# Decoder trunk on one core: up-projection panels taken in pairs, three products split once more, and four of the inner weight sums made on VectorE

## What is computed

```python
def swiglu(u, w_up, w_down):
    h = u @ w_up
    a, b = jnp.split(h, 2, axis=-1)
    return (jax.nn.silu(a) * b) @ w_down

u = rmsnorm(x, ng[0]) * (1.0 + sc1) + sh1
x = x + 0.5 * g1 * swiglu(u, P['w_ffn_up'][l, 0], P['w_ffn_down'][l, 0])
```

## Time and profile before

| | us |
|---|---|
| median of 3 runs | 3175.61 |
| lowest and highest | 3175.28 to 3176.03 |
| the profiled execution | 3176.12 |
| its span in the trace | 3174.4 |
| TensorE busy | 3132.2 |
| VectorE busy | 1169.0 |
| GpSimd busy | 856.6 |

### The profile page before, as it was taken

One profiled execution on the slowest core, in us unless ns is written; L12 is line 12 of the kernel. 1 busy time (PEld: TensorE's weight loads), 2 busy tenths in 40 slices (PEclk: granted clock), 3 DMA queues, 4 the chain that ended last, 5 costly groups with the idle time before them and its releaser, 6 DMA issues.

```text
span 3174.4 us, 42750 instructions
## 1 busy us (share of the span) xinstructions
PE 3132.2 (99%) x17722; PEld 2483.5 (78%) x17722; DVE 1169.0 (37%) x2229; ACT 421.1 (13%) x806; POOL 856.6 (27%) x749
## 2 busy tenths in 40 slices
PE   7999999999999999999999999999999999999999
PEld 5777887678777878888877778876787778788887
DVE  3223432453233463344232233224533244633432
ACT  2000001212111120000010000023021111200000
POOL 2333431210000334334333334302100003344442
PEclk9999999999999999999999999999999999999999
DMA  6544323541111223332234443234311113222221
GB/s 244 196 174 171 127 74 107 161 136 40 51 51 58 90 79 115 112 112 81 86 120 170 176 169 116 74 119 147 126 53 51 34 58 106 77 80 80 80 83 65
DMA packets 73504, 337.43 MB, mean 106 GB/s; under 512 B 10592, under 2 KB 27744, under 8 KB 40288
## 3 DMA queue, kind: packets, MB, share of 16 engines
q1 hardware_dynamic: 63936, 312.03, 27.1%
q0 software_dynamic: 6816, 18.88, 2.0%
q10 hardware_dynamic: 2560, 3.80, 0.3%
HBM read 326.55 MB, written 6.02 MB: 105 GB/s over the span
## 4 chain that ended last, share of the span: by engine, by line
PE 97%; DVE 2%; ACT 1%; DMA 1%; issue 0%; SPq 0%; DVEq 0%; ACTq 0%
PE ps L702 96%; DVE ws L1729 1%; ACT ws L1450 0%; DMA lp<-params 0%; ACT u L1450 0%; DMA ring<-w_ada 0%; DVE u L1729 0%; DVE proj L1729 0%; DVE masked_room L2104 0%; PE ps L762 0%; DVE x L1732 0%; PE ps L1277 0%; DVE masked_room L1729 0%; DVE masked_room L1732 0%; PE ps L1164 0%
## 5 line engine op out<-in xcount | busy, mean ns | idle before, releaser
L702 PE MATMUL ps<-u,ring 128*128 128x272 f32 x4608 | 1145.4, 398 | 10.9 <-ACT u L1450 9.3
L702 PEld LDWEIGHTS ps<-u,ring 128*128 128x128 f32 x4608 | 858.1, 190 | 227.3 <-issue 45.6
L1729 DVE TENSOR_TENSOR ws<-ws,ps 128x272 f32<-128x272 f32 (+2 forms) x778 | 346.6, 451 | 1488.9 <-PE ps L702 1482.1
L665 POOL TENSOR_TENSOR masked_room<-ring 128x512 f32<-128x512 f32 (+1 forms) x76 | 95.8, 1260 | 1277.9 <-DVE pause L2430 651.6
L702 PE MATMUL ps<-y,ring 128*128 128x272 f32 x1376 | 350.8, 393 | 0.0
L1450 ACT ACTIVATE ws<-ps 128x272 f32<-128x272 f32 (+1 forms) x398 | 154.9, 396 | 1316.0 <-PE ps L702 1315.4
L702 PE MATMUL ps<-y,masked_room 128*128 128x272 f32 x1296 | 315.9, 393 | 2.8 <-DVE ws L1729 2.8
L702 PE MATMUL ps<-y,ws 128*128 128x272 f32 x1296 | 315.7, 393 | 0.0
L702 PEld LDWEIGHTS ps<-y,ring 128*128 128x128 f32 x1376 | 261.4, 190 | 54.3 <-DVE proj L1729 0.7
L702 PEld LDWEIGHTS ps<-y,masked_room 128*128 128x128 f32 x1296 | 245.6, 190 | 55.7 <-issue 5.3
L702 PEld LDWEIGHTS ps<-y,ws 128*128 128x128 f32 x1296 | 246.0, 190 | 51.9 <-issue 1.6
(11 more groups left out here) (201 smaller groups left out, 2543.4 us busy)
## 6 DMA issues: line engine op xcount, KB each, us to landing
ring<-w_up SPq DMA_DIRECT2D x88, 1024.0 KB, 4.8
ring<-w_ada SPq DMA_DIRECT2D x72, 1024.0 KB, 4.8
ring<-w_down SPq DMA_DIRECT2D x32, 1024.0 KB, 4.7
ring<-w_gate SPq DMA_DIRECT2D x32, 1024.0 KB, 4.8
ring<-w_in SPq DMA_DIRECT2D x22, 1024.0 KB, 4.8
ws<-cache SPq DMA_DIRECT2D x128, 128.0 KB, 3.1
ws<-cache POOLq DMA_DIRECT2D x128, 128.0 KB, 3.4
ring<-w_down SPq DMA_DIRECT2D x16, 768.0 KB, 4.1
```

The lines of the kernel that those rows point to most:

```text
L665: nc.gpsimd.tensor_tensor(sums[:, 0], a21, a22, ALU.add).then_inc(w_sums.sem, 1)
L702: return nc.tensor.matmul(out, lhsT, rhs, start=start, stop=stop, skip_group_check=skip)
L1729: return V.tensor_tensor(out, a, b, op)
```

## The change

Panels 0, 1 and 18 to 21 stay as they were. The 16 between become 8 pairs (r = 1 to 8, `PAIRS`). In a pair eight products stay as they are, with both panels' M1, M2, M5 and M3 (a, b). The other three (six, seven, four, the old M6, M7 and M4 of both panels) are each taken as one product of 512 x 256 weights against 512 x 272 tokens, and that is split once more: seven inner products of 256 x 128 against 256 x 136, 2 matmuls each. Each is done in a front (four inner products) and a rear (three), with one of the eight products between.

- The inner token sums are made once a feed-forward by GpSimd (`inner_token_sums`, 12 instructions, into `proj`).
- The weight sums S1 to S4 of both panels (8 instructions of 512 elements a pair) and the inner weight sums of six and seven (4 of 256 elements each) are made by GpSimd (`pair_block_sums`). S3 and S4 are written over parts of the panel in the ring.
- The inner weight sums of four, the product with raw weights, are made by VectorE (`raw_sums`, 4 instructions of 256 elements), ordered behind step seven and ahead of the adds of M5.
- VectorE adds each split product together with seven instructions (`step`) and writes hidden values two tiles at a time.
- A modulation panel no longer takes a slot of the ring: it has a room of its own (`side`), and its matmuls stand at four places of a pair. Chunks are done in pairs 1 to 7 (f = 0) and in pairs 2 and 3 of the first layer's f = 1.
- A ring slot of a pair is free when its M3 has ended, no longer after that product's first matmul.
- The first hidden sums are made during the last four panels, four instructions in each.

The core of the diff:

```diff
+                def pair_block_sums(f, r):
+                    blocks = pair_blocks(f, r)
...
+                        pair_sums(pool, l, f, r - 1, "S4b")
+                    pair_sums(pool, l, f, r, "S1b")
+                    for a, (a11, a12, a21, a22) in enumerate(blocks):
+                        nc.gpsimd.tensor_tensor(pair_s2[:, a], pair_s1[:, r % 2, a], a11, ALU.subtract)\
+                            .then_inc(pr_pool.sem, 1)
+                    pair_sums(pool, l, f, r, "S2b")
+                    inner_sums(f, r, "6", [in6[:, i] for i in range(4)], pair_s2[:, 0], pair_s2[:, 1])
...
+                    for a, (a11, a12, a21, a22) in enumerate(blocks):
+                        nc.gpsimd.tensor_tensor(a21, a11, a21, ALU.subtract).then_inc(pr_pool.sem, 1)
...
+                        pair_pe(pool, l, f, r - 1, "7.3")
+                    pair_sums(pool, l, f, r, "S3b")
+                    inner_sums(f, r, "7", [inner_room(in7, i) for i in range(4)], blocks[0][2], blocks[1][2])
...
+                        pair_pe(pool, l, f, r - 1, "4.3")
+                    if r < PAIRS:
+                        first_pair_sums(f, r + 1)
+                    for a, (a11, a12, a21, a22) in enumerate(blocks):
+                        pair_pe(pool, l, f, r, ("M2a", "M2b")[a])
+                        nc.gpsimd.tensor_tensor(a12, a12, pair_s2[:, a], ALU.subtract).then_inc(pr_pool.sem, 1)
```

```diff
+                    side_modulation(l, f, r, 1)
+                    pair_sums(pe_, l, f, r, "7s4")
+                    pair_dve(pe_, l, f, r, "6.7")
+                    seven_[0]()
...
+                    side_modulation(l, f, r, 2)
+                    pair_dve(pe_, l, f, r, "4s4")
+                    if first:
+                        pe_.wait_ge(in_sums.sem, in_sums.upto(l, 12 * f + 12))
+                    pair_dve(pe_, l, f, r, "7.7")
+                    four[0]()
+                    pair_sums(pe_, l, f, r, "S4a")
+                    pair_dve(pe_, l, f, r, "c22_a")
+                    plain(2, raw(0, 4, 0), tok(4, HALF), False, part)
+                    four[1]()
+                    side_modulation(l, f, r, 3)
+                    pair_sums(pe_, l, f, r, "S4b")
+                    pair_dve(pe_, l, f, r, "c22_b")
+                    plain(5, raw(1, 4, 0), tok(4, HALF), False, part)
```

```diff
+                    def raw_sums(r):
+                        slots = [panel_wait(dve, l, f"up{n}", 2 * r + a) for a in range(2)]
+                        (top0, top1), (low0, low1) = [
+                            [ring[:, s, :].rearrange("p (k m) -> p k m", k=8)[:, k:k + 2, P:256] for k in (4, 6)]
+                            for s in slots]
+                        room = [inner_room(in4, i) for i in range(4)]
...
+                            pair_pe(dve, l, n, r - 1, "4.3")
+                        tt_(room[0], low0, low1, ADD).then_inc(pr_dve.sem, 1)
+                        tt_(room[2], top0, low0, SUB).then_inc(pr_dve.sem, 1)
+                        pair_dve(dve, l, n, r, "4s1")
+                        tt_(room[1], room[0], top0, SUB).then_inc(pr_dve.sem, 1)
+                        pair_dve(dve, l, n, r, "4s2")
+                        tt_(room[3], top1, room[1], SUB).then_inc(pr_dve.sem, 1)
...
+                    step("7", pair_second, pair_third)
+                    before = chunk_of(l, n, r - 1)
...
+                        keep_modulation(l + n, before)
...
+                    raw_sums(r)
+                    pair_dve(dve, l, n, r, "7.7")
+                    for a in range(2):
+                        pair_pe(dve, l, n, r, ("M5a", "M5b")[a])
+                        tt_(half(pair_c22, a), half(pair_third, a), ps[:, 2 + 3 * a, 0:HALF], ADD).then_inc(pr_dve.sem, 1)
```

More of the change, by code:

```diff
@@ L163, with single, singles, chunk_of @@
[L163 to L169, removed]
+PAIRS = 8
+SINGLE = FT - 2 * PAIRS
+QUARTER = HALF // 2
+def single(q):
+    return q if q < 2 else q - 2 * PAIRS
+def singles():
+    return [q for q in range(FT) if q < 2 or q >= 2 + 2 * PAIRS]
+def chunk_of(l, f, r):
+    if f == 0:
+        return r + 1 if 1 <= r <= 7 else None
+    return r - 2 if l + 1 < DEPTH and r in (2, 3) else None
@@ new lines, in side_number @@
+def side_number(l, f, r, k):
+    before = [(a, b, c) for a in range(DEPTH) for b in range(2) for c in range(1, PAIRS + 1)
+              if (a, b, c) < (l, f, r) and chunk_of(a, b, c) is not None]
+    return CHUNK * len(before) + k + 1
+PAIR_PE = {n: i + 1 for i, n in enumerate(
+    ("M1a", "M1b", "6.1", "6.2", "M2a", "6.3", "M2b", "7.1", "7.2", "M5a", "7.3", "M5b", "4.1", "4.2", "4.3"))}
+PAIR_ACT = {n: i + 1 for i, n in enumerate(("first_a", "first_b", "gate1_a", "gate1_b", "gate2_a", "gate2_b"))}
@@ L672, in weight_sums @@
                 def weight_sums(f):
-                    for q in range(FT):
+                    for q in singles():
                         if f and q == 0:
@@ L777, in ffn @@
                             sum_squares(l, 0)
-                        modulation(l, panel(l, "ada", n), n)
+                        modulation(l, ring[:, panel(l, "ada", n), :], n, part)
                         if n % CHUNK == CHUNK - 1:
@@ L790, in product @@
                     m.then_inc(wi_pe.sem, 1)
-                for q in range(FT):
-                    place, unit, sums_at = up_place(l, f, q), f * FT + q, 4 * unit_of(f"up{f}", q)
+                for q in singles():
+                    place, unit, sums_at = q, f * SINGLE + single(q), 4 * unit_of(f"up{f}", single(q))
+                    if q == 2 + 2 * PAIRS:
+                        for r in range(1, PAIRS + 1):
+                            pair(r)
                     s = load_number(l, f"up{f}", place) % R
@@ L1901, in products @@
+                for q in singles():
+                    if q == 2 + 2 * PAIRS:
+                        for r in range(1, PAIRS + 1):
+                            pair(r)
+                    unit, by, bz = n * SINGLE + single(q), 3 * (q % 2) + 1, 3 * (q % 2) + 2
                     def products(k):
```

358 lines of the change are left out of this document (284 added, 74 removed).

## The result

| | before | after |
|---|---|---|
| median of the runs, us | 3175.82 | 3285.47 |
| lowest to highest, us | 3175.28 to 3177.51 | 3270.27 to 3293.79 |
| profiled execution, us (span) | 3176.1 (3174.4) | 3293.79 (3292.1) |
| mean granted TensorE clock, profiled | 0.998 | 0.979 |

The changed kernel takes 1.0338 times as long (95% interval 1.0309 to 1.0366), 110 us more. Forecast were 83 us more, 3258.6 us, with a range of 3200 to 3315. Its runs spread far more than those of before, and the spread follows the granted clock: 3270.27 us at 0.987, 3285.80 at 0.982, 3285.13 at 0.981, 3293.79 at 0.979.

What follows compares the result with a forecast made beforehand. The prediction took TensorE's own pace to bound the kernel. Its terms -40 (split), +3 (modulation panels), +100 (wait for the four sums) and +20 (clock) gave +83 on 3175.6, so 3258.6 us, range 3215 to 3315 with turns.

Steps and rivals of the forecast that it cites:

- Part 1: Inner split of three products a pair, 136-column records at 116 ns each: TensorE work falls by 40 us.
- Rival (d): 136-column records cost TensorE what 272-column ones do: +264 in place of -40, about 3440 us; chance 0.03.
- Part 2: Modulation panels in their own buffer: single panels cost +3 us, late side loads 0 (bound 32 us).
- Part 3: VectorE's extra adds and GpSimd's extra sums stay hidden behind TensorE's products: no cost.
- Part 4: Four front waits for VectorE's four weight sums, slowed by turns with GpSimd: +100 us, bounds 27 and 135.
- (a): VectorE's four sums don't meet GpSimd's: 3166 us, or 3138 if TensorE doesn't wait at all; chance 0.12.
- (b): VectorE waits one turn, then keeps GpSimd out until all four sums are through: 3177 us; chance 0.05.
- Rival (c): Turns, but cheaper: the four sums fall on GpSimd's short inner sums, no clock loss: 3202 us; chance 0.09.
- Part 5: TensorE's granted clock falls to half after waits ahead of four front: +20 us, bounds 0 and 48.

Runs made afterwards that it cites:

- e7_gpsimd_loads: Changed kernel with four's inner weight sums made by GpSimd, and mask and parameter loads moved from panel 12 to 18: 3142.97 us.
- e2_start: Changed kernel with VectorE's four sums moved to the pair's start, ahead of step six: 3152.59 us, ratio 0.992 to the kernel before.
- e3_yield: Changed kernel with GpSimd held from the next pair's sums until VectorE's fourth sum is there: 3171.76 us, ratio 0.9982 to the kernel before.
- e5_middle: Changed kernel with VectorE's four sums moved between step six and step seven: 3153.91 us, ratio 0.9927 to the kernel before.
- e6_start_loads: e2_start with the mask and parameter loads moved from panel 12 to panel 18: 3143.49 us, ratio 0.9896 to the kernel before.

## Why the prediction was right, point by point

The sign, the place and the mechanism were right and the time fell in the range; forecast were +83, measured +110 (median) and +118 (the profiled execution). By its own steps, for the profiled execution:

| step | forecast, us | measured, us | read from |
|---|---|---|---|
| 1 inner split | -40 | -40 | 136-column records |
| 2 modulation singles | +3 | +3 | not measured by itself |
| 2 side panels late | 0 | +5 | waits for `ws<-w_ada` |
| 3 more adds and sums hidden | 0 | 0 | no other wait |
| 4 wait for the four sums | +100 | +93 | how late the 32 four fronts are |
| 5 clock | +20 | +57 | what remains; 56 read behind the gaps |

**Part 1** holds: eight 136-column records start between 2895.63 and 2896.56, 0.116 us each, the value taken. That the split pays is shown by e7_gpsimd_loads, where 34 of the 37 us are there. Rival (d) falls.

**Part 2**: the singles' 3 us were not measured apart, and fit the sum. Side panels come late twice, for 3.1 us behind the loads of the masks and parameters and for 1.7 behind those of the other layer's parameters. I had held the panel's 4.8 us of landing time against the 5.1 us between two uses and left out what else goes through the same queue: the masks and parameters in one stage and the parameters in another. The bound of 32 us covered it.

**Part 3** holds. No step of the pair other than four front has a wait for VectorE or GpSimd beyond those of before (95.5 us in all against 6.1 before, 89.4 of the difference ahead of four front). Adds of one input from PSUM are not touched by GpSimd: all 96 adds of 408 elements take 0.58 us, 54 of them while one of its sums runs, as predicted from the slope.

**Part 4** holds in its mechanism, and by e2_start and e3_yield it is shown: away from GpSimd's sums, or with GpSimd held, the sums take 0.42 us. Rivals (a) and (b) fall. By size: the sixteen pairs with panels are 2.8 us late in the mean (forecast 2.75), the twelve without 3.6 (4.25), the last ones 1.3 (1.2), together 45 + 43 + 5 = 93. The step that was mis-sized is the turn of the second sum in a pair without panels: I let it wait for S3a, 1.43 us, but it went in beside the short inner sums, so that two sums took 1.32 us. Rival (c) had that idea and spread it over all four; only two of four fall on short sums, since the third and fourth meet S3a and S3b (with panels it is the first two that meet them). The Trainium skill (SBUF — State Buffer, "Who interferes with whom") says that an instruction of VectorE with at most one SBUF input, outside the modes that use both ports, doesn't contend with GpSimd, and that one with two contends with a GpSimd instruction that reads SBUF. Its words on the whole instruction, which the prediction takes over, stand there for the modes that use both ports. The trace agrees in both halves, 0.58 us for 408 elements from PSUM and SBUF beside 0.42 or 1.48 for 256 elements from SBUF alone.

**Part 5** is the term that failed. I took 1 us for each long wait and 0.5 for each short one, since I assumed that part of the half-clock stretch would fall on the wait itself. The rows show otherwise: of 6.8 us at the lower level 1.0 lies in the wait, and the rest in four front and M3a. Over all pairs 123 us at the lower level go with these gaps, and 14 of them lie in the waits. What four fronts and M3a lose behind the gaps is 33 us in the twelve pairs without panels (2.7 each) and 23 in the sixteen with (1.8 in most, and next to nothing in the four where the clock didn't fall): 56, and what remains of the profiled execution's +118 after the other steps is 57. At the median run, +110, the remainder is 49, and filling the wait gave 42 of that back. The upper bound, 48 us, rested on the one stretch of the trace of before, 3.5 us at half level. In the pairs with panels nearly every stretch is as long as that one; in eleven of the twelve without it is twice as long, 6.8 us, and this is why the bound was too low. That the two errors, -7 and +37, partly cancel is luck, and it is luck that the time, 27 us above the forecast, stayed in the range with a term that passed its own bound.

What stays open: I didn't try whether the clock would also hold with fewer matmuls in the wait. Why four of the sixteen gaps with panels passed without a fall of the clock, although they are no shorter than others behind which it fell (2.5 to 2.7 us), no run here shows. The remainders of 49 and 57 us differ by run, as the clock does, and of the changed kernel only one execution was profiled.

## What to carry to other kernels

A sum over SBUF inputs on VectorE is cheap or three times as dear by where GpSimd stands at that moment: before giving VectorE such work ahead of a waiting TensorE, lay both engines' instructions side by side in time, and put the work where its inputs are there and slack lies behind it (e2_start, e5_middle), not at the latest place where it still seems in time. A gap of some 3 us in TensorE's stream mostly costs twice (24 of 28 here), once as a wait and once as half clock behind it; price both, and look at the product behind the gap, not only at the gap. And of a transfer that just comes in time, list all that is issued on its queue between two uses.

## What the runs showed of the hardware

- Turns are not fixed in length. VectorE's two sums beside GpSimd's sums of 256 elements took 1.32 us together; beside sums of 512 elements most took 1.37 to 1.50 each. GpSimd pays too: its two S3 sums took 2.84 us in place of 2.50.
- The half-level clock comes with a delay and stays. It fell some 2.3 us into a gap of 3.35 us and stayed for 6.8 us, a loss of 2.9 us of products; behind a gap of 2.67 us, at 125 us, the first eight 136-column records still run at nearly full pace (1.19 us) and those behind them slowly (1.78), a loss of 1.8; behind another gap of 2.67 us, at 193 us, the clock didn't fall; behind 0.78 us (e3_yield) it didn't either. In both of these four front takes 1.96 us, 0.1 more than without a gap.
- Idle time filled with matmuls that nobody needs made the kernel 42 us faster than waiting. It is no substitute for taking the wait away (e6_start_loads is another 100 us faster).
- Two kernels with the same work in other places differ in spread: 23 us between the runs of the changed kernel, 4 us or less in both of the last two, which go with clocks of 0.979 to 0.987 and 0.997 to 0.998.
